# Split out projections, an earlier split of weights, and a spread spatial norm in a two-block transformer kernel

## The reference

```
y = g0*(ret @ w_br_ret) + g1*(dsa @ w_br_dsa) + g2*(gl @ w_br_gla)
y = y @ w_out[l]
x = x + gate * rms_norm(y, post_norm[l])
```

## Time and profile before

| | |
|---|---|
| median of 3 executions | 1120.31 us (1120.24 to 1121.68) |
| the profiled execution, its time | 1122.27 us |
| the profiled execution, its span | 1120.5 us |
| busy: PE, DVE, ACT, POOL | 1075.9, 539.7, 425.4, 96.2 us |
| granted TensorE clock, mean | 0.997 |

### The profile page before, as it was taken

The page is one execution under the profiler, slowest core; times in us unless marked ns, Lnnn a source line. Parts: engine busy times, 40 slices in busy tenths (PEclk is TensorE's granted clock), DMA queues, the critical chain, the costliest instruction groups (busy, mean ns, idle before and its releaser), DMA issues.

```text
span 1120.5 us, 12855 instructions
## 1 busy us (share of the span) xinstructions
PE 1075.9 (96%) x4942; PEld 711.8 (64%) x4942; DVE 539.7 (48%) x1109; ACT 425.4 (38%) x886; POOL 96.2 (9%) x115
## 2 busy tenths in 40 slices
PE   4999999999999999999999999999999999999997
PEld 2687775554445877865544447777667888646553
DVE  2439766454325297752223434234654646144743
ACT  2436546330015365463230044244443524334741
POOL 3005110000000032110000000310000001212000
PEclk9999999999999999999999999999999999999999
DMA  9644432666524354425547425242252113432000
GB/s 389 248 178 157 192 143 84 225 229 266 204 100 151 113 225 150 151 99 209 218 174 285 180 89 212 80 160 84 76 225 106 70 38 138 182 131 113 1 1 37
DMA packets 13740, 171.25 MB, mean 153 GB/s; under 512 B 1504, under 2 KB 1760, under 8 KB 3056
## 3 DMA queue, kind: packets, MB, share of 16 engines
q1 hardware_dynamic: 12944, 167.77, 39.3%
q10 hardware_dynamic: 736, 2.65, 0.6%
HBM read 169.37 MB, written 1.05 MB: 152 GB/s over the span
## 4 chain that ended last, share of the span: by engine, by line
PE 81%; DVE 9%; ACT 6%; DMA 2%; issue 2%; ACTq 0%; DVEq 0%
PE bank L721 18%; PE bank L743 12%; PE bank L1017 7%; PE bank L1059 7%; PE bank L1106 6%; PE bank L713 5%; PE bank L1065 5%; PE bank L1243 2%; PE bank L821 2%; PE bank L1320 2%; DVE wlo L2074 2%; PE bank L676 2%; PE bank L684 2%; DMA X<-in_x 1%; PE bank L1308 1%
## 5 line engine op out<-in xcount | busy, mean ns | idle before, releaser
L721 PE MATMUL bank<-ring,hT 128*128 128x512 f32 (+1 forms) x576 | 243.5, 578 | 1.1 <-ACT retqkv L1356 0.6
L721 PEld LDWEIGHTS bank<-ring,hT 128*128 128x128 f32 x576 | 107.3, 190 | 120.0 <-issue 114.0
L2074 DVE TENSOR_TENSOR wlo<-ring,whi 128x512 fp32r<-128x512 f32 x120 | 89.0, 767 | 40.5 <-ACT whi L1432 40.3
L743 PE MATMUL bank<-whi,xhi 128*128 128x512 f32 (+1 forms) x256 | 99.1, 387 | 6.6 <-DVE wlo L2074 4.9
L1432 ACT ACTIVATE whi<-ring 128x512 fp32r<-128x512 f32 x120 | 72.7, 630 | 64.2 <-PE bank L743 64.1
L743 PE MATMUL bank<-wlo,xhi 128*128 128x512 f32 (+1 forms) x256 | 96.4, 377 | 0.0
L743 PE MATMUL bank<-whi,xlo 128*128 128x512 f32 (+1 forms) x256 | 96.4, 377 | 0.0
L743 PEld LDWEIGHTS bank<-whi,xhi 128*128 128x128 f32 x256 | 48.1, 188 | 21.5 <-issue 7.7
L1065 PE MATMUL bank<-ring,hT 128*128 128x256 f32 (+2 forms) x224 | 57.9, 418 | 3.3 <-ACT hT L1399 2.3
L1356 ACT ACTIVATE G<-bank 128x512 f32<-128x512 f32 x24 | 14.3, 596 | 119.8 <-PE bank L721 119.8
L1017 PE MATMUL bank<-ring,X 128*128 128x512 f32 x128 | 55.9, 595 | 0.0
(11 more groups left out here) (396 smaller groups left out, 1781.8 us busy)
## 6 DMA issues: line engine op xcount, KB each, us to landing
ring<-in_weights SPq DMA_DIRECT2D x73, 2048.0 KB, 8.4
ring<-in_weights SPq DMA_DIRECT2D x5, 1024.0 KB, 5.0
ring<-in_weights SPq DMA_DIRECT2D x2, 1360.0 KB, 7.7
ring<-in_weights SPq DMA_DIRECT2D x1, 1536.0 KB, 8.3
kk<-in_k SPq DMA_DIRECT2D x1, 1120.0 KB, 7.9
X<-in_x ACTq DMA_DIRECT2D x1, 1024.0 KB, 15.5
kc<-in_k ACTq DMA_DIRECT2D x1, 1024.0 KB, 11.8
X<-in_context SPq DMA_DIRECT2D x1, 1024.0 KB, 10.8
```

The costliest lines, as they stand in the source:

```text
L721: mm = pe.matmul(ps[:, 0:width], hT[:, k, t * P:(t + 1) * P], ring[:, slot, k * stride + w0:k * stride + w0 + width], start=(k == 0), stop ...
L743: mm = pe.matmul(o[:, 0:width], a, b[:, q % BUFFERS, at], start=(k == 0 and m == 0), stop=(k == KD - 1 and m == 2))
L2074: dve.tensor_tensor(wlo1[:, q % BUFFERS, :], piece1(q)[2], whi1[:, q % BUFFERS, :], ALU.subtract).then_inc(event("lo1_ready"), 1)
```

## The change

The diff without its unchanged lines:

```diff
--- before.py
+++ after.py
@@ -328,6 +328,7 @@
+        y_high = first_of("y_high", [P, KD, S], F32R)
@@ -363,6 +364,7 @@
+        out_high = first_of("out_high", [P, 2, KD, 512], F32R)
@@ -524,6 +526,12 @@
+        def out_piece(h, i):
+
+            slot = (len(CH0) + [n for n, _ in CH1].index(f"out{h}")) % RING
+            c = slice(i * 1024, (i + 1) * 1024)
+            return (ring[:, slot, c], out_high[:, h, 2 * i:2 * i + 2, :].rearrange("p k c -> p (k c)"), ring_low[:, slot, c])
+
@@ -1021,25 +1029,34 @@
-                for h in range(2):
-                    ps = begin(u, f"gb{h}")
-                    done(u, f"gb{h}", pe.matmul(ps[:, :], ones[:], DG[:, 4 * h:4 * h + 4, :], start=True, stop=True))
...
+                    for h in range(2) if t == 0 else ():
+                        ps = begin(u, f"gb{h}")
+                        done(u, f"gb{h}", pe.matmul(ps[:, :], ones[:], DG[:, 4 * h:4 * h + 4, :], start=True, stop=True))
...
-                        project(u, f"out{t}{h}", slots[h], t, 512)
-                        if (t, h) == (1, 0) and l + 1 < DEPTH:
-                            turn_x1(l + 1, 0)
-                        elif (t, h) == (1, 0):
-                            turn_x2(le, 1, E_ORDER[0])
-                            turn_x2(le, 2, E_ORDER[1])
+                        ps = begin(u, f"out{t}{h}")
+                        for k in range(KD):
+                            if (t, h, k) == (1, 1, KD // 2):
+                                if l + 1 < DEPTH:
+                                    turn_x1(l + 1, 0)
+                                else:
+                                    turn_x2(le, 1, E_ORDER[0])
+                                    turn_x2(le, 2, E_ORDER[1])
+                            if k % 2 == 0 and t == 0:
+                                pe.wait_ge(event("out_low"), 8 * l + 4 * h + k // 2 + 1)
+                            hi, low = y_high[:, k, t * P:(t + 1) * P], xlo1[:, k, t * P:(t + 1) * P]
+                            whole, rest = out_high[:, h, k, :], ring_low[:, slots[h], k * 512:(k + 1) * 512]
+                            for m, (a, b) in enumerate(((hi, whole), (hi, rest), (low, whole))):
+                                mm = pe.matmul(ps[:, :], a, b, start=(k == 0 and m == 0), stop=(k == KD - 1 and m == 2))
+                        done(u, f"out{t}{h}", mm)
@@ -1458,25 +1475,25 @@
-                high(16, 20)
-
+                high(16, 23)
+                for t in range(TT):
+                    copy_out(u, f"ret_qk{t}", retqkv[:, t, 0:512])
+                high(23, 24)
...
-                settle()
-                act.activation(LG[:], AZ[:], ACT.Ln, bias=1.0).then_inc(event("lg_ready"), 1)
-                high(20, 24)
-                for t in range(TT):
-                    copy_out(u, f"ret_qk{t}", retqkv[:, t, 0:512])
...
-                high(24, 32)
+                high(24, 27)
+                settle()
+                act.activation(LG[:], AZ[:], ACT.Ln, bias=1.0).then_inc(event("lg_ready"), 1)
+                high(27, 31)
...
-                high(32, 36)
+                high(31, 39)
...
-                high(36, 40)
+                high(39, 40)
@@ -1566,9 +1583,17 @@
-                    copy_out(u, f"gb{h}", gpb[:, h * 512:(h + 1) * 512])
+                    arrived(act, CH1, [n for n, _ in CH1].index(f"out{h}"), len(CH0), l)
+                    for i in range(4):
+                        w, whole, _ = out_piece(h, i)
+                        act.activation(whole, w, ACT.Copy).then_inc(event("out_high"), 1)
-                    copy_out(u, f"yT{t}0", hT[:, 0:4, t * P:(t + 1) * P])
+                    for h in range(2):
+                        ps = filled(act, u, f"yT{t}{h}")
+                        act.activation(y_high[:, 4 * h:4 * h + 4, t * P:(t + 1) * P], ps[:, :].rearrange("p (k c) -> p k c", k=4),
+                                       ACT.Copy).then_inc(event("y_high_ready"), 1)
+                    for h in range(2) if t == 0 else ():
+                        copy_out(u, f"gb{h}", gpb[:, h * 512:(h + 1) * 512])
@@ -1706,7 +1731,7 @@
-                for j, n in {4: ((1, 0), (1, 1)), 5: ((1, 2), (1, 3)), 11: ((2, 0), (2, 1)), 12: ((2, 2), (2, 3))}.get(g, ()):
+                for j, n in {4: ((1, 0), (1, 1)), 5: ((1, 2), (1, 3)), 10: ((2, 0), (2, 1)), 11: ((2, 2), (2, 3))}.get(g, ()):
@@ -2121,8 +2146,7 @@
-                        n_ = len(pieces) // (TOPK // 8)
-                        low(pieces[0] + i * n_, pieces[0] + (i + 1) * n_)
+                        low(pieces[0] + i * len(pieces) * 8 // TOPK, pieces[0] + (i + 1) * len(pieces) * 8 // TOPK)
@@ -2138,7 +2162,8 @@
-                scores(1, range(20, 36))
+                low(20, 23)
+                scores(1, range(23, 36))
@@ -2285,6 +2310,13 @@
+                def out_rest(h):
+
+                    for i in range(4):
+                        w, whole, rest = out_piece(h, i)
+                        dve.wait_ge(event("out_high"), 8 * l + 4 * h + i + 1)
+                        dve.tensor_tensor(rest, w, whole, ALU.subtract).then_inc(event("out_low"), 1)
+
@@ -2306,6 +2338,8 @@
+                    if b == 1:
+                        out_rest(0)
@@ -2315,8 +2349,13 @@
-                    ps = filled(dve, u, f"yT{t}1")
-                    dve.tensor_copy(hT[:, 4:8, t * P:(t + 1) * P], ps[:, :].rearrange("p (k c) -> p k c", k=4)).then_inc(free(u, f"yT{t}1"), 1)
+                    for h in range(2):
+                        dve.wait_ge(event("y_high_ready"), (l * TT + t) * 2 + h + 1)
+                        ps = filled(dve, u, f"yT{t}{h}")
+                        c = slice(t * P, (t + 1) * P)
+                        dve.tensor_tensor(xlo1[:, 4 * h:4 * h + 4, c], ps[:, :].rearrange("p (k c) -> p k c", k=4),
+                                          y_high[:, 4 * h:4 * h + 4, c], ALU.subtract).then_inc(free(u, f"yT{t}{h}"), 1)
+                out_rest(1)
@@ -2413,7 +2452,8 @@
-            for t in range(NT):
+            def spatial_norm(t):
+
@@ -2488,6 +2528,8 @@
+                if g < NT:
+                    spatial_norm(g)
@@ -2506,10 +2548,10 @@
-                for j, n in {5: ((1, 0), (1, 1)), 6: ((1, 2), (1, 3)), 11: ((2, 0), (2, 1)), 12: ((2, 2), (2, 3))}.get(g, ()):
+                for j, n in {5: ((1, 0), (1, 1)), 6: ((1, 2), (1, 3)), 11: ((2, 0), (2, 1), (2, 2)), 12: ((2, 3),)}.get(g, ()):
-                if g in (8, 11, 13):
-                    e_gated({8: 0, 11: 1, 13: 2}[g])
+                if g in (8, 10, 13):
+                    e_gated({8: 0, 10: 1, 13: 2}[g])
```

## The result

The changed kernel takes 1104.26 us (median of 4 executions, 1103.01 to 1106.44) against 1120.84 us (median of 4). The ratio is 0.985, with a 95% interval of 0.9833 to 0.9867: 16.6 us less, where 18.7 less was forecast. The profiled execution took 1105.05 us with a span of 1103.3 us, 17.2 us less than the span before.

What follows compares the result with a forecast made beforehand. PE was taken as the bound, busy 1075.9 of 1120.5 us. Terms 10.3 + 4.2 + 3.2 + 1.0 = 18.7 us took the profiled 1122.27 to 1103.6, and the median to 1101.6, range 1096.5 to 1108.5.

Steps and rivals of the forecast that it cites:

- Out projections, forecast 10.3: Eight out projections in split form, 1.24 us less each, 9.9, plus two waits of 0.2 gone: 10.3 us less.
- less tight than feared: Second layer's `out1` weights: ACT done at 643.1 against a first need at about 643.3, just in time.
- Projection phase, forecast 4.2: `ret_v` and `gla_v` up to `ret_g`: both outer waits go, 2.1 us earlier per layer, 4.2 us less (0 to 7.8).
- head at 95.7, slowed by half, to 98.4: Projection phase: DVE's head of the second selection, beside POOL's rotation, slowed by half and done at 98.4.
- the count piece by piece: Projection phase: low 23 ready at 100.6, PE at full pace from 107.9 to 120.2, at `ret_g` at 121.1.
- The loss of 0.9 us a layer: Projection phase if DVE blocks fully behind POOL: about 0.9 us lost a layer, sum 6.0 us smaller.
- Grid layer, forecast 3.2 and 1.0: Wait and slow clock after `e_g01` go, 4.1 less 0.9 at spatial unit: 3.2; wait at 885.05 goes: 1.0.
- Rival 1: Projection phase: the rotation takes all its gain, DVE being the bound; 14.5 us less, 1105.8; chance 0.11.
- Rival 2: Grid layer: wait over 2 us returns at the spatial unit with slow clock; gain 0, 1105.8; chance 0.08.
- Rival 3: Everything that waits in the changed places goes: 23.7 us less, 1096.6; chance 0.06.
- Rival 4: Out projections: `out1` lands late, stopping its parts and the turned tiles; slower, 1122 at 21 us landing; chance 0.03.
- rival 5: Out projections: split form isn't faster, price nearly that of the plain form; gain 8.8, 1111.5; chance 0.04.

Runs made afterwards that it cites:

- the run with the old place: Changed kernel with the turn of the next normed tile back ahead of `out11`, as in the kernel before; 1107.83 us, ratio 0.9874.
- the out projections alone: Kernel before with only the split out projections of the change; 1111.1 us, ratio 0.9908.
- the late norm: Changed kernel with the spatial norm of all four tiles in step 3 of the grid layer; 1109.8 us, ratio 0.9905.

## Why the prediction was right, and where it was not

The forecast was 1101.6 us, the result is 1104.3. Of the difference of 2.7 us, 1.5 lie in the terms (18.7 forecast for the span, 17.2 found). The other 1.2 lie in the step from the profiled execution to the median: I took 1.96 us off, as before, and it is 0.79 here. The profiled executions differ by up to 2 us ahead of the first changed place, so neither number was one to build on. That the terms came as close as 1.5 us is in part luck: the out projections gave 1.3 us more than forecast, which covers most of the 1.6 that the projection phase gave less.

**Out projections, forecast 10.3.** Found 5.63 us in the first layer and 5.98 in the second, 11.6. The mechanism was right: no wait for a high or low part, the turn covered, the tile-1 wait unchanged. A projection is 5.59 us (23.15 us less the turn of 0.79, by four), and the plain one, counted in the same way, was 6.89, so 1.30 instead of 1.24. The new order of transposes and gate gave 0.35 us in each layer instead of 0.1, and the turn in the middle of `out11` is a little shorter. `out1` was less tight than feared: in the second layer ACT began its parts at 629.04, was done at 632.9, and waited 2.2 us for the turn of `Y`. The later place of the turn was needed, as the run with the old place shows.

**Projection phase, forecast 4.2.** Found 1.28 and 1.31 us, 2.6. This is the step that failed: "head at 95.7, slowed by half, to 98.4". Three multiply-adds beside POOL took 4.27 us, 2.8 times their 1.53, so low part 23 was ready at 101.7 and not 100.6. After it the count piece by piece was near (24.85 us for the stretch; the count gives 24.0, from the 96.2 at which `ret_v` starts without the wait to 120.2). I had priced the head by a guess, when the earlier trace rows has only low parts beside the rotation.

I had also misread those low parts. A line that merges two records gives their mean at best, and the 1.19 us of the earlier trace rows is no low part's time. Record by record, the two parts of each line are very unequal; the kernel before first, then the changed kernel with two of its low parts, a multiply-add, and POOL:

```profile
98.99 0.68 DVE L2074 TENSOR_TENSOR wlo<-ring,whi 128x512 fp32r<-128x512 f32 x1
...
99.59 1.78 DVE L2074 TENSOR_TENSOR wlo<-ring,whi 128x512 fp32r<-128x512 f32 x1
```

```profile
102.64 0.80 DVE L2099 TENSOR_TENSOR wlo<-ring,whi 128x512 fp32r<-128x512 f32 x1
...
103.36 1.77 DVE L2099 TENSOR_TENSOR wlo<-ring,whi 128x512 fp32r<-128x512 f32 x1
...
97.20 1.40 DVE L2137 SCALAR_TENSOR_TENSOR sc<-G,idx,sc 128x256 f32<-128x256 f32 x1
...
102.85 1.74 POOL L1871 TENSOR_TENSOR retqkv<-Y 128x512 f32<-128x512 f32 x1
```

POOL's operations end at 100.83 in the kernel before, and at 98.32, 102.89 and 104.59 in the changed one. The low parts that began before these ends were done 0.54 to 0.55 us behind them (101.37, 103.44, 105.13), and the multiply-add 0.28 us behind (98.60); alone they take 0.68 and 0.48. The first layers of all twelve traces with the rotation say the same: 0.54 to 0.58 us for every low part and 0.28 to 0.29 for every multiply-add that begins inside one of its operations. So each waited for POOL's whole operation. POOL was slower too: 1.29 us for its first operation, begun ahead of the multiply-adds, 1.45 to 1.48 among them, 1.65 to 1.75 among low parts.

The Trainium skill's page SBUF — State Buffer, section "Who interferes with whom", has a DVE instruction with two SBUF inputs contend with a GpSimd instruction that reads SBUF. Its section "Summary: rules for kernel authors" has the second of the two fully block until the first finishes. The trace agrees with both, in place and in size; the prediction said otherwise of the size because of that mean.

The loss of 0.9 us a layer that I had worked out for a full block was still far too large, where 1.3 were gained. Only about one low part in two is held for long, because POOL moves on during DVE's rounds of the selection. In all, DVE lost 4.0 us to the rotation in the changed kernel and 3.7 in the kernel before (the records beside it, less what they take alone). So the change made the rotation hardly dearer for DVE. It moved the loss ahead of low part 23, for which PE then waited.

**Grid layer, forecast 3.2 and 1.0.** The first is 3.3: step 2 without wait and at full clock, and 1.04 us at the spatial unit, where 1.15 was said. The second is 0.27. The wait of 1.01 us at the first `eout` went, but `e_gated(1)`, a step earlier on DVE, now holds back the `mod_out` of `ada3`, and the gate rows wait 0.73 us for it. I had counted the idle time of DVE in that step and not asked what stands behind the moved work in DVE's list. The run with `e_gated(1)` behind that `mod_out` has neither wait.

**Not in the forecast:** the load in the latent layer comes 0.6 us later in relation to PE, a wait for `PT` in the second layer costs 0.3 more (0.91 us against 0.63, and 0.91 with the out projections alone, so it comes with them), and the start was 0.3 earlier. Together: 11.6 + 2.6 + 3.3 + 0.3 - 0.9 + 0.3 = 17.2.

**The rivals.** Rival 1 (the rotation takes all of the phase's gain) was true in part: the rotation took 1.6 us more than forecast, of the 4.2, and the chance of 0.11 was for all of it. Rival 2 (a wait of over 2 us returns at the spatial unit, with the slow clock) didn't come, but the mechanism exists, as the late norm showed. Rival 3 (all these waits go) is out: PE waits 1.56, 1.04 and 0.73 us in these places. Rival 4 is out, since PE waits for no high part, and rival 5, since a projection takes 5.59 us.

## What to carry to other kernels

When work moves earlier, price it beside what runs there now, on every engine, and ask what stands behind it in its own engine's list: both losses here came from that. Before pricing from a merged line of a profile, ask for its records one by one. Helper work on a shared resource should begin as late as its reader allows; DVE lost about 3 us wherever the rotation lay behind the head (4.0 beside it), and PE lost 3.0, 1.5, 0.7 or nothing by how far DVE was ahead. When PE's work gets shorter, move what it covered by as much.

## What the runs showed of the hardware

- Three DVE multiply-adds of 128x256 with both tensors in SBUF took 1.52 us alone and 4.27 beside POOL's products. Each of them, and each low part, waited for the end of the POOL operation in which it began (0.48 us became 1.40, 0.68 became up to 1.78). MAX8 stayed at 0.42 beside them, as the changed kernel's DVE and POOL show:

```profile
101.72 0.42 DVE L2145 MAX8 m<-wk 128x8 f32<-128x256 f32 x1
...
101.24 1.65 POOL L1870 TENSOR_TENSOR retqkv<-Y 128x512 f32<-128x512 f32 x1
```

- After one and the same wait of PE (2.51 us) the clock stayed at the 1.2 GHz level for 3.3 us in one execution and for over 5.9 in another. Behind PE's waits of 1.56, 1.58 and 1.04 us in the changed kernel it stayed at 1.00, in windows with columns as above:

```profile
101.80:106.00 4.20, 4.13 (x16) 2.77 (x17) 4.13 (x12) 2.32 (x4) 2.79 (x2) 1.00 0.02 4
...
675.86:681.00 5.14, 5.14 (x23) 4.41 (x24) 5.14 (x5) 4.70 (x12) 0.00 (x0) 1.00 0.13 29
792.21:797.00 4.79, 4.59 (x31) 2.68 (x32) 2.46 (x6) 2.62 (x6) 0.00 (x0) 1.00 0.40 111
```

- What comes ahead of 77 us varies by 2 us between executions. It isn't the clock alone: before and after differ there by 0.28 us, while the granted clock from 22 to 30 us is 1.00 in the one and 0.59 in the other. The cause wasn't looked for.
